# Merged pairs of norms, a renormed x written back later, and weight tiles split at other places around each norm

## The reference

```python
def first_block(x, ...):
    for l in range(DEPTH):
        x = x + 0.5 * swiglu_ffn(rmsnorm(x, ffn1_norm[l]), ...)
        x = x + mixer(rmsnorm(x, mix_norm[l]), ...)
        x = x + 0.5 * swiglu_ffn(rmsnorm(x, ffn2_norm[l]), ...)
        x = rmsnorm(x, final_norm[l])
    return x

def second_block(x, c, ...):
    c_act = jax.nn.silu(c)
    for i in range(DEPTH):
        mod = c_act @ mod_w[i] + mod_b[i]
        sh_m, sc_m, g_m, sh_f, sc_f, g_f = jnp.split(mod[:, None, :], 6, axis=-1)
        h = rms_norm(x, norm_mix_pre[i]) * (1.0 + sc_m) + sh_m
        y = mixer_ab(h, ...) if i % 2 == 0 else mixer_c(h, ...)
        x = x + (1.0 + g_m) * rms_norm(y, norm_mix_post[i])
        h = rms_norm(x, norm_ffn_pre[i]) * (1.0 + sc_f) + sh_f
        y = conv_ffn(h, ...)
        x = x + (1.0 + g_f) * rms_norm(y, norm_ffn_post[i])
    return x
```

## Time and profile before

| | |
|---|---|
| median of 3 runs | 2442.98 us (2442.26 to 2448.7) |
| profiled execution, its own time | 2443.44 us |
| its span | 2441.6 us |
| TensorE busy | 2298.9 us, 94% of the span |
| VectorE busy | 1727.7 us, 71% |
| ScalarE busy | 1192.4 us, 49% |
| chain that ended last | 88% TensorE, 8% VectorE, 3% ScalarE |

### The profile page before, as it was taken

How to read it: one execution, slowest core, us unless ns; L and a number is a source line. 1 busy time by engine, 2 the same in 40 slices (tenths; PEclk the granted TensorE clock), 3 DMA queues, 4 the chain that set the end, 5 groups by cost and what they waited for, 6 DMA issues and landing times.

```text
span 2441.6 us, 45856 instructions
## 1 busy us (share of the span) xinstructions
PE 2298.9 (94%) x18202; PEld 2238.6 (92%) x18202; DVE 1727.7 (71%) x2811; ACT 1192.4 (49%) x1752; POOL 98.2 (4%) x196
## 2 busy tenths in 40 slices
PE   7999999989998999999998999899898999798997
PEld 6999999989998999999988999789887999797997
DVE  6667899767667766899866766586445766666766
ACT  4444444554444444454454544445454565444564
POOL 0000020000000000021000000000000000000000
PEclk8999999999999999999999999997799999998999
DMA  7775555235775777465324677343112455353552
GB/s 282 235 239 193 178 174 168 79 130 187 238 236 183 255 234 235 160 185 169 130 87 147 233 241 238 109 154 104 52 62 78 142 184 183 110 173 112 181 180 94
DMA packets 113503, 412.26 MB, mean 169 GB/s; under 512 B 13792, under 2 KB 13920, under 8 KB 112992
## 3 DMA queue, kind: packets, MB, share of 16 engines
q1 hardware_dynamic: 96192, 352.26, 42.8%
q0 software_dynamic: 16896, 56.64, 7.5%
q10 hardware_dynamic: 288, 1.57, 0.2%
HBM read 403.07 MB, written 1.05 MB: 166 GB/s over the span
## 4 chain that ended last, share of the span: by engine, by line
PE 88%; DVE 8%; ACT 3%; issue 1%; DMA 0%; DVEq 0%; ACTq 0%; SPq 0%
PE bank L503 86%; DVE w_lo L1370 2%; PE bank L643 1%; DVE arena L1533 1%; ACT w_hi L981 1%; DVE rinv L1404 1%; DVE work L1407 1%; DVE work L1439 1%; DVE h_lo L1398 0%; ACT rinv L1002 0%; ACT work L1123 0%; DVE rinv L1436 0%; ACT arena L1262 0%; ACT work L1000 0%; DMA tabs<-shape_tables 0%
## 5 line engine op out<-in xcount | busy, mean ns | idle before, releaser
L503 PE MATMUL bank<-h_hi,w_hi 128*128 128x256 f32 x3968 | 1151.2, 291 | 62.9 <-ACT h_hi L1008 27.9
L503 PE MATMUL bank<-h_hi,w_lo 128*128 128x256 f32 x3968 | 1135.1, 287 | 0.0
L503 PE MATMUL bank<-h_lo,w_hi 128*128 128x256 f32 x3968 | 1102.8, 284 | 0.0
L1370 DVE TENSOR_TENSOR w_lo<-w_raw,w_hi 128x1024 fp32r<-128x1024 f32 x663 | 808.6, 1222 | 373.5 <-ACT w_hi L981 367.1
L981 ACT ACTIVATE w_hi<-w_raw 128x1024 fp32r<-128x1024 f32 x663 | 699.8, 1057 | 638.7 <-PE bank L503 632.9
L503 PEld LDWEIGHTS bank<-h_hi,w_hi 128*128 128x128 f32 x3968 | 777.1, 196 | 80.9 <-issue 54.1
L503 PEld LDWEIGHTS bank<-h_hi,w_lo 128*128 128x128 f32 x3968 | 777.1, 196 | 0.0
L503 PEld LDWEIGHTS bank<-h_lo,w_hi 128*128 128x128 f32 x3968 | 755.3, 193 | 0.4 <-issue 0.2
L503 PE MATMUL bank<-hid_hi,w_hi 128*128 128x256 f32 (+1 forms) x1104 | 314.0, 284 | 9.4 <-ACT arena L1188 2.9
L503 PE MATMUL bank<-hid_lo,w_hi 128*128 128x256 f32 (+1 forms) x1104 | 312.2, 283 | 0.0
L503 PE MATMUL bank<-hid_hi,w_lo 128*128 128x256 f32 (+1 forms) x1104 | 311.9, 283 | 0.0
(11 more groups left out here) (217 smaller groups left out, 1887.3 us busy)
## 6 DMA issues: line engine op xcount, KB each, us to landing
w_raw<-weights SPq DMA_DIRECT2D x663, 512.0 KB, 3.4
mod_w_buf<-mod_w POOLq DMA_DIRECT2D x96, 512.0 KB, 4.8
mod_w_buf<-arena POOLq DMA_DIRECT2D x96, 64.0 KB, 3.7
tabs<-shape_tables SPq DMA_DIRECT2D x1, 1682.0 KB, 14.4
work<-v_bias ACTq DMA_DIRECT2D x2, 768.0 KB, 4.4
x<-x_fm SPq DMA_DIRECT2D x1, 1024.0 KB, 4.8
out_fm<-x SPq DMA_DIRECT2D x1, 1024.0 KB, 3.9
vecs<-vectors SPq DMA_DIRECT2D x1, 712.0 KB, 7.4
```

What stands on the lines that cost most here:

```text
L503: ins = pe.matmul(o, lhs, rhs, start=start, stop=stop, skip_group_check=share)
L1370: v.tensor_tensor(w_lo[:, n % SPLIT, :], w_raw[:, n % RAW, :], w_hi[:, n % SPLIT, :].bitcast(F32), ALU.subtract).then_inc(lo_ready[n % SPL ...
```

## The change

1. At both seams the two norms become one. VectorE's `norm_pair` scales x by the product of both gains (`pair_gain`) and one root. TensorE's `mean_pair` makes the sum for it with the columns `pair_mean` = (gain squared + eps) / 1024, which four small VectorE operations in `first_vectors` make, and directly after it the plain sum of squares for the first norm of the two, into another bank (`square_used` counts its eight steps).
2. x itself must still be renormed (`ffn_steps` gets `fresh` for that, and VectorE waits for ScalarE's copy, `x_back`, before its convolution). At the first seam VectorE does it inside the next FFN (`new_root` after step 3, `renew` in steps 4 and 5). At the second it does it at the start of the mixer, by `in_order` into `work` in token order, and ScalarE copies `work` to x (after `renewed`). `in_order` also writes the second seam's normed tiles, already in token order.
3. `mod_cols` and `mod_vector` of the seams move behind the first pair of weight tiles of the next stage.
4. In every norm ScalarE rounds the third weight tile right behind the root, and VectorE splits it right behind the `h_lo` parts; where a post-norm adds to x, VectorE splits it behind that addition. At the start three tiles are rounded and split ahead of the root.
5. At the end of each FFN VectorE splits the last tile behind the update of x, and steps 0 to 2 take two `mod_tiles` each instead of steps 0 and 1, so that the last step has none.
6. `normed_pair` has the loops over tiles and columns swapped: four products on each `h_hi` tile as it comes.

```diff
--- before.py
+++ after.py
@@ -550,11 +557,10 @@
 
 
                 tiles = [slot(), slot()]
-                for c, n in enumerate(tiles):
-                    for kt in range(KT):
-                        if c == 0:
-                            pe.wait_ge(h_high, w.next(h_high))
-                        at = slice(kt * P, kt * P + P)
+                for kt in range(KT):
+                    pe.wait_ge(h_high, w.next(h_high))
+                    at = slice(kt * P, kt * P + P)
+                    for c, n in enumerate(tiles):
                         mm(half(b, c), w_hi[:, n, at], h_hi[:, kt, :], (c, kt) == (0, 0), False, share=True)
...
@@ -581,7 +587,18 @@
...
-            def ffn(mod=False):
+            def mean_pair(l):
+
+                if l == 0:
+                    pe.wait_ge(pair_mean_ready, w.next(pair_mean_ready))
+                for kt in range(KT):
+                    pe.wait_ge(sq_ready, w.next(sq_ready))
+                    mm(half(6, 0), pair_mean[:, l, kt:kt + 1].broadcast_to([P, P]), work[:, kt, :], kt == 0, kt == KT - 1,
+                       stat_full if kt == KT - 1 else None)
+                for kt in range(KT):
+                    mm(half(3, 0), tab("mean_all"), work[:, kt, :], kt == 0, kt == KT - 1, square_used)
+
+            def ffn(mod=False, first=None):
 
                 def down(j, par, last=False):
                     n = slot()
@@ -592,6 +609,8 @@
...
+                if first is not None:
+                    first()
                 column_pair(None, None)
                 down(0, 0)
                 t0, p0 = state["tile"], state["pair"]
@@ -770,6 +789,7 @@
...
             def recurrent_nsa_mixer():
                 column_pair(h_ready)
+                mod_cols()
                 column_pair()
...
@@ -936,18 +956,18 @@
...
+            mean_squares()
             for l in range(DEPTH):
-                mean_squares()
-                ffn(True)
+                ffn(True, mod_cols if l else None)
                 mean_squares()
                 mod_cols()
                 first_mixer(l)
                 mean_squares()
                 ffn(True)
-                mean_squares()
-                mod_cols()
+                mean_pair(l)
             for l in range(DEPTH):
-                mean_squares()
+                if l:
+                    mean_squares()
                 recurrent_nsa_mixer() if l == 0 else short_conv_mixer()
...
@@ -993,21 +1013,41 @@
...
-            def squares(src, ready):
+            def squares(src, ready, tiles=None):
...
                     act_f(work[:, kt, :], src[:, kt, :], ACT.Square).then_inc(sq_ready, 1)
+                if tiles is not None:
+                    high_parts(tiles)
                 act.wait_ge(stat_full, w.next(stat_full))
                 act_f(rinv[:, :], half(6, 0), ACT.Sqrt, bias=tab("eps")).then_inc(root_ready, 1)
-
-            def norm(ready, shift):
-                squares(x, ready)
+                high_parts(state["tile"] + 2)
+
+            def norm(ready, shift, tiles=None):
...
+
+            def norm_pair(shift, o):
+                for kt in range(KT):
+                    if kt % 2 == 0:
+                        act.wait_ge(x_ready, w.next(x_ready))
+                    act_f(work[:, kt, :], x[:, kt, :], ACT.Square).then_inc(sq_ready, 1)
+                act.wait_ge(stat_full, w.next(stat_full))
+                act_f(rinv[:, :], half(6, 0), ACT.Sqrt, bias=tab("eps_sq")).then_inc(root_ready, 1)
+                high_parts(state["tile"] + 2)
...
+                act.wait_ge(h_ready, w.last(h_ready))
+                act.wait_ge(square_used, w.next(square_used, KT))
+                act_f(o, half(3, 0), ACT.Sqrt, bias=tab("eps")).then_inc(root_ready, 1)
...
@@ -1164,6 +1204,10 @@
...
                     b, free = next_pair()
                     act_f(zk[:, kind, :], bank[b][:, :], ACT.Copy).then_inc(free, 1)
+                act.wait_ge(renewed, w.next(renewed, KT))
+                for k in range(0, KT, 4):
+                    ins = act_f(x[:, k:k + 4, :], work[:, k:k + 4, :], ACT.Copy)
+                ins.then_inc(x_back, 1)
...
@@ -1298,27 +1342,21 @@
...
             for l in range(DEPTH):
-                norm(None if l == 0 else x_ready, None)
                 if l == 0:
+                    norm(None, None, 2)
                     act.wait_ge(vecs_loaded, w.next(vecs_loaded, 16))
-                    high_parts(2)
                     first_vectors()
                 ffn_steps(plain_step)
                 first_mixer(l)
                 norm(res_pair, None)
                 ffn_steps(plain_step)
-                squares(x, x_ready)
-
-            act.wait_ge(scaled, w.next(scaled, KT))
...
+                if l == DEPTH - 1:
+                    act.wait_ge(mod_ready, w.next(mod_ready, MOD_PARTS))
+                norm_pair(*((modv[:, 0, 0, :], gate_a[:, 0, :]) if l == DEPTH - 1 else (None, work[:, 0, :])))
             for l in range(DEPTH):
-                act.wait_ge(mod_ready, w.next(mod_ready, MOD_PARTS))
-                norm(x_ready if l else None, modv[:, l, 0, :])
+                if l:
+                    act.wait_ge(mod_ready, w.next(mod_ready, MOD_PARTS))
+                    norm(x_ready, modv[:, l, 0, :])
...
@@ -1408,19 +1454,45 @@
...
                 for kt in range(KT):
                     h_low(kt, 0.0 if shift is None else shift[:, kt:kt + 1])
-
-            def final_norm(l):
-
-                gain = vec("final_norm", l, 0, KT)
+                low_parts(state["tile"] + 2)
+
+            def norm_pair(l, shift):
+
+                gain = pair_gain[:, l, :]
                 dve.wait_ge(root_ready, w.next(root_ready))
                 v.reciprocal(rinv[:, :], rinv[:, :]).then_inc(dve_link, 1)
                 dve.wait_ge(dve_link, w.next(dve_link))
                 for kt in range(KT):
...
+                    dve.wait_ge(square_used, w.next(square_used))
+                    if l == 0:
+                        v.scalar_tensor_tensor(work[:, kt, :], x[:, kt, :], gain[:, kt:kt + 1], rinv[:, :],
+                                               ALU.mult, ALU.mult).then_inc(scaled, 1)
+                    else:
+                        in_order(kt, gain, rinv[:, :], scaled)
+                for kt in range(KT):
+                    h_low(kt, 0.0 if shift is None else shift[:, kt:kt + 1])
+                low_parts(state["tile"] + 2)
+
+            def in_order(kt, gain, root, done):
+
+                o = work[:, kt, :].rearrange("p (a h l) -> p h a l", h=2, l=2)
+                for r in range(2):
+                    at = slice(r * P, (r + 1) * P)
+                    ins = v.scalar_tensor_tensor(o[:, r], x[:, kt, at].rearrange("p (a l) -> p a l", l=2), gain[:, kt:kt + 1],
+                                                 root[:, at].rearrange("p (a l) -> p a l", l=2), ALU.mult, ALU.mult)
+                ins.then_inc(done, 1)
+
+            def new_root(root):
+
+                dve.wait_ge(root_ready, w.next(root_ready))
+                v.reciprocal(root, root).then_inc(dve_link, 1)
+                dve.wait_ge(dve_link, w.next(dve_link))
+
+            def renew(tiles):
+
+                gain, root = vec("final_norm", 0, 0, KT), work[:, 0, :]
+                for kt in tiles:
+                    v.scalar_tensor_tensor(x[:, kt, :], x[:, kt, :], gain[:, kt:kt + 1], root, ALU.mult, ALU.mult)
...
@@ -1493,13 +1566,20 @@
...
                         low_parts(t0 + 3 * j + 3)
                         hidden(j % 2)
-                        low_parts(min(t0 + 3 * j + 5, t0 + 3 * FT + 1))
+                        low_parts(min(t0 + 3 * j + 5, t0 + 3 * FT))
                 else:
                     for j in range(FT):
                         hidden(j % 2)
-                        low_parts(min(t0 + 3 * j + 3, t0 + 3 * FT + 1))
-                        mod_tiles(2 if j < 2 else 1)
-                        low_parts(min(t0 + 3 * j + 5, t0 + 3 * FT + 1))
+                        if fresh and j == 0:
+                            mod_vector()
+                        low_parts(t0 + 3 * j + 3)
+                        if j < FT - 1:
+                            mod_tiles(2 if j < 3 else 1)
+                        low_parts(min(t0 + 3 * j + 5, t0 + 3 * FT))
+                        if fresh and j == 3:
+                            new_root(work[:, 0, :])
+                        if fresh and j in (4, 5):
+                            renew(range((j - 4) * KT // 2, (j - 3) * KT // 2))
                         if j - 2 in (2 * MOD_TURNS[0], 2 * sum(MOD_TURNS[:2])):
                             mod_vector()
...
@@ -1512,6 +1592,7 @@
...
+                low_parts(t0 + 3 * FT + 1)
...
@@ -1717,7 +1798,13 @@
...
             def recurrent_nsa_mixer():
-                skip_pairs(2)
+                skip_pairs(1)
+                mod_vector()
+                new_root(gate_a[:, 0, :])
+                for kt in range(KT):
+                    if kt == KT // 2:
```

(14 more changed lines are left out.)

46 lines of the change are left out of this document (29 added, 17 removed).

## The result

The changed kernel took 2422.95 us, median of 4 runs (2420.17 to 2424.59). The kernel before took 2444.41 in the same comparison (2442.26 to 2448.7, 4 runs). The ratio is 0.9909, interval 0.9891 to 0.9926. A second comparison gave 0.9907. The gain of the medians is 21.5 us, that of the two profiled spans 18.8; 25.8 was forecast, to 2417.6, with 2408 to 2429 as the range. In the later comparisons the kernel before has 42 runs with a median of 2448.07 us (2442.44 to 2454.49), and only 7 of them took less than the 2443.44 us of the record of before that is read here; the gain over runs is 22 to 24 us, more than the two spans show.

What follows compares the result with a forecast made beforehand. TensorE, 88% of the chain, was taken as the bound, so only its idle time or lower clock matters. 9.0 - 1.84 + 9.2 + 4.0 + 1.0 + 1.2 + 3.2 = 25.8 off 2443.4 gave 2417.6 us, range 2412 to 2424 (neighbouring cases 2408 to 2429).

Steps and rivals of the forecast that it cites:

- Seams: Block 1's layer 0 end and block 1's end, two norms merged: 9.0 less 1.84 us, and net 9.2.
- R to T: At each seam, first root's end to TensorE finishing the first column pair: 18.1 to 9.1, 24.8 to 11.1 us.
- The wait in the second mixer: Behind the second seam, TensorE waits 2.2 us for the seventh weight tile, rounded only after ScalarE's copy of x.
- Ends of FFNs: TensorE's 0.8 us idle before the sum of squares goes at five FFN ends: 4.0 us in all.
- Third tile in the first mixers: Norms before the two first mixers: earlier rounding and split of the third weight tile saves 0.5 us each, 1.0.
- Loop order at block 2's later norms: Three later norms of block 2: four products per tile use the full clock longer; 0.4, 0.8 and 0, sum 1.2 us.
- Start: Kernel start: three weight tiles split ahead of the root, first product at 19.7 us; gain 3.2, bounds 1 and 7.
- the wait of 0.9: At the start, TensorE waits 0.9 us and not 0.2 for the fourth weight tile's split.
- Cover: Next FFN's steps 3 to 5: VectorE's 2.4 us slack per step hides postponed renorming; cost zero, 5.0 without it.
- Slower: Block 1's FFNs: a third pair of modulation loads in a row comes late, VectorE holds weight splits; 2451 us, chance 0.03.
- no change: All put-off renorming returns on the path, the start gives nothing, two clock dips come; 2438 us, chance 0.04.
- less is won: VectorE paces both seams, four clock dips of 1.5 us, start gives 1, second mixer loses 5; 2428 us, chance 0.15.

Runs made afterwards that it cites:

- experiment 3: The changed kernel with the old loop order (columns outside, tiles inside) in the first pair; ratio to the kernel before 0.9900.
- experiment 5: The changed kernel with the old start, first three weight tiles rounded and split behind the first norm; ratio to the kernel before 0.9903, median 2423.92 us.
- Experiments 8 to 11: Constant products in TensorE's waits, three times on the changed kernel with x copied later, once (third) on the kernel before; ratios 0.9853, 0.9826, 0.9963, 0.982.
- experiment 9: The changed kernel with x copied later and constant products in the norms, 28 instead of 44 ahead of second sums; 2406.48 us, ratio 0.9826.
- experiments 8 and 9: The changed kernel with x copied later and constant products in the norms, 44 then 28 ahead of second sums; 2411.96 and 2406.48 us.

## Why the prediction was right, and what it missed

The direction, the mechanism of the large terms and the time inside the range were right. The terms one by one, from the two records:

- *Seams.* R to T: 18.1 to 9.0 (forecast 9.1) and 24.8 to 10.6 (11.1). `mod_cols` cost its 1.84 twice. The wait in the second mixer was 1.44, not 2.7. Together 18.2 instead of 16.4. The granted clock was 1.00 from 769 to 785 and from 1529 to 1545, as assumed.
- *Ends of FFNs.* All five waits of 0.80 are gone: 4.0, as forecast.
- *Third tile in the first mixers.* Waits of 0.38 and 0.42 are gone: 0.8 for 1.0.
- *Loop order at block 2's later norms.* Forecast 1.2. Only one wait there changed, from 1.08 to 0.70, and experiment 3 finds no difference in time: this term was wrong. Why it was is open; of the three norms two began at half clock in after, where the prediction had one (0.55 us for the first product at 1879.44 and 2094.54, 0.36 at 2215.00).
- *Start.* 3.9 at the fourth weight tile for 3.2, because the wait of 0.9 did not come; experiment 5 confirms the idle time (3.5) but not the time.
- *Cover.* `new_root` and `renew` cost nothing: no wait appears in the FFN's steps 3 to 5.
- *Slower, no change.* VectorE's waits for modulation loads rose from 0.5 to 2.0 us in all, and TensorE waited for none of them; of the work put off only the 1.44 came back.

By the terms as measured the sum is about 27 us. Idle time is 22.9 of it: at the start 3.7, in the seams with their first sums 15.6, at the other three ends 2.4, for `w_lo` 1.2. The other 4 or so are products in the seams that ran at low clock before and at full clock after (the second seam's sum took 5.50 us and takes 3.62). The 2 us that are left of the 24.9 of idle time are no gain: they are waits of the first mixers for `h_lo` (2.36 and 2.26 before, 1.15 and 1.55 after) that slower products filled.

The two spans are only 18.8 us apart, so some 8 us of the 27 are lost elsewhere. The sum has no term for that: it priced each product outside the seams as before, and the granted clock only inside them. The lead of after over before at the same instruction shows where it went. It is 5.2 us ahead of the small products of layer 0 (480.47 and 475.23), 2.1 behind them and 4.0 at the end of that mixer's next stretch (549.06 and 545.07); 12.9 and then 9.8 at the same products in layer 1 (1245.18 and 1232.28, 1283.83 and 1274.00); 20.6 at the first of block 2's second sums of squares (1889.88 and 1869.26) and 18.3 at the weight tile at 1910.04 and 1891.71; 17.9 and then 15.4 between two waits at 2187.70 and 2221.25 (clock 0.94 before, 0.88 after); and, behind the third of these sums (6.69 us before, 5.63 after), 18.8 to the end. That a lower clock is the cause of these losses in the records is shown, by the same instructions at two clocks.

That the change brings a lower clock with it is not shown. The record of before is one of the shorter of that kernel's runs, at a mean clock of 0.964; its runs have 0.958 to 0.965, on average 0.9616 (42 runs), and those of the changed kernel 0.962 to 0.964, on average 0.9626 (8 runs). At the same 0.962 seventeen runs of before took 2446.1 to 2448.8 us and five of after 2423.8 to 2424.9, about 23 us less. The drop in the first mixers stands in every record with the new splits, but there is only one record of before to hold against them. What is missing is a record of before from a run near its median.

This also says which part of the forecast 2417.6 was off. Measured is 2422.95, 5.3 more. The base was 2443.4, from that one record and a median of three runs; the later 42 runs have their median 4.7 us higher, and 2448.1 - 25.8 is 2422.3. Of the gain itself, 25.8 were forecast and 22 to 24 came over the runs.

Experiments 8 to 11 show that the clock can be raised by products that compute nothing and that this saves time, but it is not the loss above that they win back (experiment 9). The rule of the Trainium skill, that activity releases the throttle (*TensorE: Matmul & The Clock Gate*, Part 1), agrees with experiments 8 and 9: the mean clock of 0.962 became 0.974 to 0.977. By itself it would also have had the change, which only fills idle time, raise the clock; between the averages above, 0.9616 and 0.9626, little of that shows.

The case "less is won" named four dips at the seams; none came there. In the records the loss was of its kind, at other places.

## What to carry to other kernels

Split a span into TensorE's idle time and its busy time for the same number of products: the first tells whether a change did what it should, the second what the clock made of it. Then look where the record lies among the runs of its kernel: here a record at 2443.4 us of a kernel whose runs have their median at 2448.1 made 24 us of gain look like 18.8. A gain of 3.5 us in idle time (experiment 5) can vanish in a time that moves by 10 us between runs, so small terms are to be judged by their rows. Where TensorE must wait between dense stretches, constant products into an unused half bank, a little shorter than the wait, gave 15 to 18 us on the changed kernel (2421.6 to 2406.5 and 2404.0), not far from what the restructuring gave, for a few lines. On the kernel before they gave 6 to 9, so this gain has to be measured anew for each kernel. Longer than the wait they cost what they overrun.

## What was not expected of the hardware

- The same 18202 products took TensorE 2298.9 to 2307.0 us in the nine records of kernels without added ones.
- A sum of squares of eight float32 products of 256 columns takes 3.6 us at full clock and up to 6.69 where most of it runs at half (clock 0.55). Three such sums stand behind an idle time of 6.8 us and on the path of the norm. They were slow in the kernel before too (5.14, 5.74 and 6.69 us), and the prediction, which priced only what the change touches, passed them over.
- Identical instructions behind the same wait of 1.4 us ran at full clock in the record of one kernel and took 38% longer in that of another (8.04 and 11.07 us), and products put into other waits, which raised the mean clock to 0.976, left them at 11.3.
